# Three groups of inner rows turned in one run, and other runs of turns joined or reordered, in a two-block transformer kernel

## The reference

```
x += 0.5 * swiglu(rmsnorm(x), w_gu, w_down)            # "f1", inner width 2816
h  = rmsnorm(x);  z = h @ w_in
y_a = u * (causal mix of layernorm(v) over 128 rows)    # 8 groups of 64
y_b = causal attention, 8 heads, from two latents:
      q = rmsnorm(c_q) @ w_uq ; k, v = rmsnorm(c_kv) @ w_ukv ; rope
y_c = attention to 256 memory rows, 4 heads of 128
x += (sum of gate_i * (y_i @ w_i)) @ w_out
x += 0.5 * swiglu(rmsnorm(x), ...)                      # "f2"
x += g1 * conv_mixer(modulate(rmsnorm(x)))              # 3-tap convolution along rows of 64
x += g2 * swiglu(modulate(rmsnorm(x)))                  # "f3"
return rmsnorm(x) * final_g
```

## Time and profile before

| | |
|---|---|
| median of three runs | 907.61 us |
| profiled execution | 906.8 us |
| its span | 905.1 us |
| VectorE busy | 615.4 us |
| ScalarE busy | 463.0 us |
| GpSimd busy | 44.7 us |
| DMA | 197.83 MB, mean 219 GB/s |

### The profile page before, as it was taken

The page is one execution under the profiler, slowest core; times in us unless marked ns, Lnnn a source line. Parts: engine busy times, 40 slices in busy tenths (PEclk is TensorE's granted clock), DMA queues, the critical chain, the costliest instruction groups (busy, mean ns, idle before and its releaser), DMA issues.

```text
span 905.1 us, 11265 instructions
## 1 busy us (share of the span) xinstructions
PE 892.7 (99%) x4210; PEld 745.4 (82%) x4210; DVE 615.4 (68%) x861; ACT 463.0 (51%) x694; POOL 44.7 (5%) x66
## 2 busy tenths in 40 slices
PE   8999999999999999999999999999999999999996
PEld 6888888888998888888888888887888788888885
DVE  6688876647558877587667777766768755555653
ACT  6665443536688466447544545354445444444440
POOL 0010000022103000000000000001000100000000
PEclk9999999999999999999999999999999999999999
DMA  9798777874554444444787777865755566555541
GB/s 366 298 344 277 272 281 279 270 229 159 175 177 171 175 175 163 163 169 156 239 276 278 280 273 277 287 229 170 249 186 173 184 224 185 187 186 185 182 145 47
DMA packets 56575, 197.83 MB, mean 219 GB/s; under 512 B 6936, under 2 KB 7880, under 8 KB 56392
## 3 DMA queue, kind: packets, MB, share of 16 engines
q1 hardware_dynamic: 55512, 195.66, 63.0%
q10 hardware_dynamic: 1008, 1.45, 0.4%
HBM read 196.01 MB, written 1.07 MB: 218 GB/s over the span
## 4 chain that ended last, share of the span: by engine, by line
PE 96%; DMA 1%; issue 1%; DVE 1%; POOL 1%; ACT 1%; POOLq 0%
PE ps L721 29%; PE ps L719 29%; PE ps L720 29%; PE ps L746 2%; PE ps L634 1%; PE ps L627 1%; DMA t_hn<-in_xT 1%; PE ps L657 1%; PE ps L845 1%; PE ps L861 1%; PE ps L803 0%; PE ps L837 0%; POOL t_sc L1684 0%; PE ps L785 0%; DMA t_acc<-in_xT 0%
## 5 line engine op out<-in xcount | busy, mean ns | idle before, releaser
L1204 DVE TENSOR_TENSOR t_wl<-t_raw,t_wh 128x1024 fp32r<-128x1024 f32 (+3 forms) x308 | 364.1, 1207 | 146.4 <-ACT t_wh L903 144.6
L903 ACT ACTIVATE t_wh<-t_raw 128x1024 fp32r<-128x1024 f32 (+3 forms) x308 | 310.7, 1043 | 142.5 <-DMA t_raw<-in_f_up 66.4
L719 PE MATMUL ps<-t_wh,t_XH 128*128 128x512 f32 (+2 forms) x640 | 250.7, 392 | 0.0
L721 PE MATMUL ps<-t_wh,t_XL 128*128 128x512 f32 (+2 forms) x640 | 247.1, 386 | 0.0
L720 PE MATMUL ps<-t_wl,t_XH 128*128 128x512 f32 (+2 forms) x640 | 246.7, 385 | 0.0
L721 PEld LDWEIGHTS ps<-t_wh,t_XL 128*128 128x128 f32 x640 | 120.1, 188 | 24.2
L720 PEld LDWEIGHTS ps<-t_wl,t_XH 128*128 128x128 f32 x640 | 120.3, 188 | 22.5
L719 PEld LDWEIGHTS ps<-t_wh,t_XH 128*128 128x128 f32 x640 | 120.2, 188 | 22.4
L719 PE MATMUL ps<-t_wh,t_YH 128*128 128x512 f32 x288 | 113.4, 394 | 0.0
L721 PE MATMUL ps<-t_wh,t_YL 128*128 128x512 f32 x288 | 112.3, 390 | 0.0
L720 PE MATMUL ps<-t_wl,t_YH 128*128 128x512 f32 x288 | 112.1, 389 | 0.0
(11 more groups left out here) (227 smaller groups left out, 625.7 us busy)
## 6 DMA issues: line engine op xcount, KB each, us to landing
t_raw<-in_f_up SPq DMA_DIRECT2D x131, 512.0 KB, 3.9
t_raw<-in_f_dn SPq DMA_DIRECT2D x66, 512.0 KB, 3.5
t_raw<-in_ada SPq DMA_DIRECT2D x48, 512.0 KB, 4.5
t_raw<-in_mkv SPq DMA_DIRECT2D x8, 512.0 KB, 3.8
t_raw<-in_ga SPq DMA_DIRECT2D x8, 512.0 KB, 3.2
t_raw<-in_gc SPq DMA_DIRECT2D x8, 512.0 KB, 3.2
t_raw<-in_gb SPq DMA_DIRECT2D x8, 512.0 KB, 3.2
t_raw<-in_wo SPq DMA_DIRECT2D x8, 512.0 KB, 3.2
```

The source lines that it names most:

```text
L719: pe.matmul(o, xh, h, start=k == 0, stop=False)
L721: x = pe.matmul(o, xl, h, start=False, stop=k == n - 1)
L903: act.activation(wh[:, m % SPL, lo:w], raw[:, n % RAW, lo:w], ACT.Copy).then_inc(hi_made, 1)
L1204: dve.tensor_tensor(wl[:, n % RAW, lo:w], raw[:, n % RAW, lo:w], wh[:, m % SPL, lo:w].bitcast(F32), ALU.subtract).then_inc(drained, 1)
```

## The change

`HELD = 3`: `hp` gets three places, and three groups are turned in one run after the third unit of groups 3, 6 and 9; the last two groups are turned in one run in `dn0`. VectorE's `hid` now waits for the turns three groups back. In the middle stage `lat_turn` of `cq` moves from unit 20 to 21 and that of `ckv` from 24 to 25, where memory steps already stand; the causal attention moves from odd units 37, 39, ... to even ones 38, 40, ..., so that its first step joins `su`; `y_turn` of a and b move one unit on. Within `mem` and `att`, the turns of the next head (`in`) now stand before the scores (`sc`). The two `gate_turn` of the second convolution half come in one run after unit 0. The host reserves 8192 instead of the default for `dynamic_dma_scratch_size`.

```diff
+HELD = 3
-                own = [("hid_turn", f, g - 2), ("hid_turn", f, g - 1)] if g and g % 2 == 0 and i == 2 else []
+                own = [("hid_turn", f, h) for h in range(g - HELD, g)] if g and g % HELD == 0 and i == 2 else []
...
-            unit(f"{f}_dn0", i, *([("hid_turn", f, 10)] if i == 2 else []), *extra.get(44 + i, ()))
+            unit(f"{f}_dn0", i, *([("hid_turn", f, h) for h in range(11 // HELD * HELD, 11)] if i == 2 else []),
+                 *extra.get(44 + i, ()))
...
-        parts = (("mem_val", k - 4), ("mem_pt", k - 3), ("mem_sc", k - 1), ("mem_in", k), ("mem_exp", k - 1))
+        parts = (("mem_val", k - 4), ("mem_pt", k - 3), ("mem_in", k), ("mem_sc", k - 1), ("mem_exp", k - 1))
...
-        parts = (("att_val", k - 4), ("att_pt", k - 3), ("att_sc", k - 1), ("att_in", k), ("att_exp", k - 1))
+        parts = (("att_val", k - 4), ("att_pt", k - 3), ("att_in", k), ("att_sc", k - 1), ("att_exp", k - 1))
...
-            20: [("lat_turn", "cq", 0), ("lat_turn", "cq", 2), ("lat_stat", "ckv")],
-            22: [("lat_row", "ckv")], 24: [("lat_turn", "ckv", 0)], 26: [("sv_mean",)],
+            21: [("lat_turn", "cq", 0), ("lat_turn", "cq", 2), ("lat_stat", "ckv")],
+            22: [("lat_row", "ckv")], 25: [("lat_turn", "ckv", 0)], 26: [("sv_mean",)],
...
-            35: [("sv_norm", 1)], 38: [("su", 0), ("su", 1)], 41: [("y_turn", "a", 0), ("y_turn", "a", 1), ("load_cond", 1)],
-            61: [("y_turn", "b", 0), ("y_turn", "b", 1)]}
+            35: [("sv_norm", 1)], 38: [("su", 0), ("su", 1)], 42: [("y_turn", "a", 0), ("y_turn", "a", 1), ("load_cond", 1)],
+            62: [("y_turn", "b", 0), ("y_turn", "b", 1)]}
...
-        side[37 + 2 * n] = side.get(37 + 2 * n, []) + att(n)
+        side[38 + 2 * n] = side.get(38 + 2 * n, []) + att(n)
...
-                unit("conv_cc1", m, *([("gate_turn", 0, m), ("gate_low", 0, m)] if m < 2 else []))
+                unit("conv_cc1", m, *([("gate_turn", 0, 0), ("gate_turn", 0, 1), ("gate_low", 0, 0), ("gate_low", 0, 1)] if m == 0 else []))
...
-            hp = sb("hp", [P, 2, 2, 256], F32, c)
+            hp = sb("hp", [P, HELD, 2, 256], F32, c)
...
-                    if g >= 2 and t == 0:
-                        dve.wait_ge(turned, place["hid", f, g - 2][1])
+                    if g >= HELD and t == 0:
+                        dve.wait_ge(turned, place["hid", f, g - HELD][1])
...
-    nc = _bacc.Bacc("TRN2", target_bir_lowering=False, num_devices=1)
+    nc = _bacc.Bacc("TRN2", target_bir_lowering=False, num_devices=1, dynamic_dma_scratch_size=8192)
```

More of the change, by code:

```diff
@@ L740, in hid_turn @@
             def hid_turn(f, g):
-                s = g % 2
+                s = g % HELD
                 b = bank(("hid", f, g), *hid_lo.at(f, g))
@@ L1315, in hid @@
                 for t in (0, 1):
-                    o, gt = hp[:, s, t, :], sg[:, s, t, :]
+                    o, gt = hp[:, g % HELD, t, :], sg[:, s, t, :]
                     up = ps[:, bank_of(f"{f}_up{g}", t), 256:512]
                     dve.wait_ge(*silu_made.at(f, g, t))
-                    if g >= 2 and t == 0:
-                        dve.wait_ge(turned, place["hid", f, g - 2][1])
+                    if g >= HELD and t == 0:
+                        dve.wait_ge(turned, place["hid", f, g - HELD][1])
                     if f == "f3":
```

## The result

The changed kernel takes 909.45 us (median of 14 runs, 909.21 to 910.35), the kernel before 907.65 us (907.28 to 908.7) beside it: a ratio of 1.0021, interval 1.0014 to 1.0028. The forecast was 907.9 us with a range from 906.7 to 909.2; the time is 1.8 us above the kernel before and above the range.

A forecast was written before the change was run, and what follows sets the result against it. TensorE was taken as the bound from end to end. Terms -0.3 (joins), -0.2 (first `att_in`), 0 and +0.76 (bank wait) gave +0.3 us: 907.1 profiled, 907.9 us as median, range 906.7 to 909.2.

The forecast's parts named there:

- Scores behind the next head's turns: Attention and memory runs ending in scores: same work in another order, 0 us (-0.1 to +0.1 for ten runs).
- The new bank wait: Run after unit 21: fifth item, the scores, waits for ScalarE's copy of the first `cq` turns, +0.76 us (0 to 1.5).
- Joins: Ten runs of turns fewer in feed-forward layers, middle stage and convolution, 0.03 us each: -0.3 us (-0.6 to -0.2).
- The first `att_in`: Attention's first step, now behind `su`, loses its 0.19 us wait for VectorE's rope of k: -0.2 us (-0.2 to 0).
- Order of items: Turns of the next head ahead of the scores in `mem` and `att`: only seams differ, 0 us.
- `ckv`: Its turns one unit later leave 0.17 us of lead before the product needing it: 0 us, at worst +0.3.
- A: Rival: scores in the run after unit 21 do not wait for a PSUM bank; 907.1 us, chance 0.14.
- B: Rival: bursts of three turns make VectorE's splits late in f1; 910.0 us, 914.1 in all nine runs; chance 0.06.
- C: Rival: constant per run of turns is larger; 907.5 us at 0.06 each, 905.8 at 0.24; chance 0.11.
- D: Rival: the 0.17 us lead of `ckv` before its product is absent; +0.3 us more, 908.2 us, chance 0.07.
- F: Rival: joined turns wait for their last inputs, so joining saves nothing; 908.2 us, chance 0.06.
- E: Rival: TensorE's clock falls to 1.2 GHz at the run after unit 21; +4 us more, 911.9 us, chance 0.02.

The follow-up runs named there:

- o3: The kernel before with only the causal attention on even units and the two `y_turn` one unit later, old order of items: 909.28 us, ratio 1.0017.
- p1: The changed kernel with the causal attention and the two `y_turn` back on their old units (attention on odd ones): 908.02 us, ratio 1.0006.
- p5: The changed kernel with only the gate steps of branches a and c moved behind the next unit's side steps: 907.92 us, ratio 1.0002.
- p6: The changed kernel with the `cq` turns last in the run after unit 21, still five items: 908.58 us, ratio 1.0011.
- o2: The kernel before with only the order within `mem` and `att` changed, next head's turns ahead of the scores: 907.90 us, ratio 1.0005.
- p2: The changed kernel with `lat_turn` of `cq` and `ckv` back after units 20 and 24: 909.13 us, ratio 1.0017.
- o1: The kernel before with only three groups at a time (`HELD = 3`) and the smaller scratch reserve: 907.54 us, ratio 0.9999.

## Why the prediction was wrong

- **The step that failed** is "Scores behind the next head's turns", where I let the exponential's bank be "one whole run on as before, since every item keeps its distance to its like", and with it the move of the attention to even units, which I priced only at its first step. TensorE's side of the distance did stay. What moved was the attention step against the gate steps in ScalarE's and VectorE's order, and that made their chain 15.4 us for two heads against TensorE's 15.0. It cost 1.6 us in two holes; o3 shows it alone (2.0 us, in the old order of items), p1 and p5 take it away in two different ways. The rows were at hand: the exponentials' starts in the kernel before. I hadn't read them, having looked at waits of TensorE only, where a chain with 1.5 us of room for two heads shows nothing.
- **The new bank wait** was right in place, mechanism and size: +0.76 forecast, 0.9 in the trace with the same two splits ahead of the copies, 0.87 between the medians of p6 and the changed kernel and 0.86 between their paths. But my rule, items of one run, was too narrow: the rotation reaches back into the run before, where scores last asks for the same copy (0.4 us in o2 and p2). That is why undoing the join alone gave 0.3 and not 0.8 in the median.
- **Joins**: forecast -0.3 for ten (0.03 each); the layers' six give 0.13, the gate pair 0.05, so 0.02 each, the lower end. The alternative of 0.24 per run, an estimate from the 81 ns that the page "TensorE: Matmul & The Clock Gate" of the Trainium skill, section "Back-to-back issue gap", has for a pair of load and matmul of 128 columns, falls here: a run of twelve turns takes 1.33 us against 0.89 for eight, 0.11 a turn, and six joins saved 0.13 us and not 1.4 (o1).
- **The first `att_in`**: -0.2, as forecast. **Order of items**: forecast 0, and 0 apart from the bank (o2). **`ckv`**: no wait at its product, as forecast.
- **Rivals**: A (no bank wait), B (burst), C (dearer runs) and D fell, though 909.45 us lies closer to B's 910.0 than to the forecast: that is chance, since no wait follows a run of twelve turns. F fell too, by the run of twelve turns and by o1. So did E: with 0.9 and 1.2 us of standing inside runs of turns and scores the clock stayed at 1.00 and the products behind kept 0.23 us. The page "TensorE: Matmul & The Clock Gate" of the Trainium skill, section "Part 4: PE-mode transpose", says of one kernel that the full clock did not engage for transposes, which would have favoured E. It is not borne out here: turns stand 0.11 us apart in the runs and twice that, 0.21, at the entry, so in the runs they too go at the higher level.
- **Sum** by what was measured: +0.9 bank, +1.6 attention, -0.2 first wait, -0.2 joins: +2.1; on the path +2.0, in the medians +1.8. Without the one missing term it is +0.5 (p5: path +0.37, median +0.4), near the forecast +0.3.

## What to carry to other kernels

When a step that several engines share moves by one place in a common order, write out each engine's sequence between two of its recurrences, before and after, and add up the handovers: the cycle through two half-idle engines (here each was busy 9.4 of the 15.4 us for two heads) can be longer than the bound engine's and shows as no wait until it is. In a rotation of buffers count places back across runs, and ask of each who empties it and what stands ahead of that in its queue. A thing that costs 0.02 us can't be harvested by moves whose slack isn't known to the microsecond: the joins that moved nothing else kept their gain, those bought by moving a step lost 0.9 and 1.6 us.

## What the runs showed of the hardware that was not expected

- A run of fp32 turns between fp32r products costs hardly more than its turns: 0.02 us a run (o1), 0.11 us a turn at eight and at twelve.
- The first products of the kernel stood 0.427 us apart, the spacing of 1.2 GHz, for twelve in a row in one execution, and 0.23 us apart in another with the same code. Ahead of them stood fourteen turns both times, 0.21 us apart in all fourteen profiles, twice the distance of later turns. The granted clock printed 1.00 for these stretches, so there the distances between starts decide. The same product in f1 started between 27.3 and 28.9 us over the fourteen profiles. In single profiles this hides differences of 1 us, so spans were not compared.
